# A two-block transformer kernel: the first weight in two halves, buffer clears off GpSimd, another order on VectorE

## The reference

```python
def reference(x, ...):
    # block 1
    h = rms_norm(x, attn_pre_g);  proj = h @ w_in            # 1024 -> 2304
    y_a = rms_norm(sliding_window_attention_with_sinks(...)) # 8 query heads, 2 key heads, ALiBi
    y_b = differential_attention(...)                        # 4 heads, two softmaxes each, lambda
    x = x + rms_norm(concat(y_a, y_b) @ w_out, attn_post_g)
    u = rms_norm(x, ffn_pre_g) @ w_up                        # 1024 -> 8192, then a causal 3-tap convolution
    x = x + rms_norm((gelu(c_gate) * c_value) @ w_down, ffn_post_g)
    # block 2, modulated by mod = silu(c) @ w_ada + b_ada    # 1024 -> 6144
    x = x + gate_mix * (concat(dilated_mixture, stick_breaking) @ w_out_2)
    x = x + gate_ffn * hierarchical_moe(...)                 # 32 experts, top 2
    return rms_norm(x, g_final)
```

## Time and profile before

| | |
|---|---|
| median of 3 runs | 1101.72 us (1100.43 to 1105.70) |
| the profiled execution | 1104.06 us; its span in the trace 1102.4 us |
| TensorE busy | 1017.5 us, 92% |
| VectorE busy | 541.0 us, 49% |
| ScalarE busy | 324.1 us, 29% |
| GpSimd busy | 80.8 us, 7% |
| HBM read | 310.32 MB, 282 GB/s over the span |
| the chain that ended last | TensorE 82%, VectorE 11%, waits for nothing shown 2%, ScalarE 2%, DMA 2% |

### The profile page before, as it was taken

How to read it: one execution, slowest core, us unless ns; L and a number is a source line. 1 busy time by engine, 2 the same in 40 slices (tenths; PEclk the granted TensorE clock), 3 DMA queues, 4 the chain that set the end, 5 groups by cost and what they waited for, 6 DMA issues and landing times.

```text
span 1102.4 us, 15139 instructions
## 1 busy us (share of the span) xinstructions
PE 1017.5 (92%) x5949; PEld 707.5 (64%) x5951; DVE 541.0 (49%) x903; ACT 324.1 (29%) x501; POOL 80.8 (7%) x111
## 2 busy tenths in 40 slices
PE   2998759999999999999988899999999999999995
PEld 2997649998999998889877544444444444433441
DVE  6556786979999996738674411111111111111113
ACT  3354516435445464527450100000000000000001
POOL 7300030101111000200010000000000000000000
PEclk9999779999999999899989899999999999999998
DMA  7316045788988864244335799799999999999991
GB/s 272 121 40 217 13 154 183 253 282 285 343 297 291 312 251 168 77 160 147 137 154 200 319 432 375 323 367 424 430 425 427 426 427 429 423 426 429 427 409 41
DMA packets 60351, 311.89 MB, mean 283 GB/s; under 512 B 4005, under 2 KB 5370, under 8 KB 47514
## 3 DMA queue, kind: packets, MB, share of 16 engines
q1 hardware_dynamic: 51728, 284.17, 65.6%
q0 software_dynamic: 7456, 26.91, 6.6%
q10 hardware_dynamic: 1130, 0.29, 0.1%
HBM read 310.32 MB, written 1.05 MB: 282 GB/s over the span
## 4 chain that ended last, share of the span: by engine, by line
PE 82%; DVE 11%; issue 2%; ACT 2%; DMA 2%; POOL 0%; DVEq 0%; POOLq 0%; SPq 0%; ACTq 0%
PE bank L741 12%; PE bank L742 11%; PE bank L743 11%; PE bank L1112 10%; PE bank L1081 10%; PE bank L1072 10%; PE bank L1023 6%; PE bank L1036 5%; DVE ring_r L1499 4%; DMA ring<-in_w_up 1%; PE bank L795 1%; PE bank L826 1%; ACT scratch L1394 1%; PE bank L731 1%; PE bank L1090 1%
## 5 line engine op out<-in xcount | busy, mean ns | idle before, releaser
L741 PE MATMUL bank<-hT_r,ring_r 128*128 128x256 f32 x744 | 215.8, 290 | 14.8 <-DVE ring_r L1499 12.7
L743 PE MATMUL bank<-hT_r,ring_r 128*128 128x256 f32 x744 | 213.0, 286 | 0.0
L1499 DVE TENSOR_TENSOR ring_r<-ring,ring_r 128x2048 fp32r<-128x2048 f32 (+1 forms) x78 | 173.7, 2262 | 18.7 <-ACT ring_r L1183 18.4
L741 PEld LDWEIGHTS bank<-hT_r,ring_r 128*128 128x128 f32 x744 | 145.3, 195 | 18.2 <-issue 16.4
L1183 ACT ACTIVATE ring_r<-ring 128x2048 fp32r<-128x2048 f32 (+1 forms) x78 | 144.1, 1890 | 43.5 <-DMA ring<-in_w_up 36.4
L742 PE MATMUL bank<-v_tok_r,ring_r 128*128 128x256 f32 x512 | 145.6, 284 | 0.0
L743 PEld LDWEIGHTS bank<-hT_r,ring_r 128*128 128x128 f32 x744 | 145.3, 195 | 0.0
L1949 DVE TENSOR_TENSOR scratch<-scratch,bank 128x512 f32<-128x512 f32 x16 | 11.0, 688 | 237.0 <-PE bank L1081 237.0
L1081 PE MATMUL bank<-ring,scratch 128*64 128x512 f32 x496 | 113.3, 595 | 0.0
L1112 PE MATMUL bank<-ring,scratch 128*64 128x512 f32 x480 | 106.3, 595 | 6.6 <-ACT scratch L1394 6.6
L1072 PE MATMUL bank<-ring,scratch 128*64 128x512 f32 x480 | 105.6, 592 | 0.0
(11 more groups left out here) (292 smaller groups left out, 1427.9 us busy)
## 6 DMA issues: line engine op xcount, KB each, us to landing
ring<-in_w_up SPq DMA_DIRECT2D x47, 2048.0 KB, 12.2
ring<-in_w_down SPq DMA_DIRECT2D x37, 2048.0 KB, 10.9
ring<-in_w_gate SPq DMA_DIRECT2D x30, 2048.0 KB, 12.6
ring<-in_w_in SPq DMA_DIRECT2D x10, 2048.0 KB, 8.3
kT<-in_w_ada POOLq DMA_DIRECT2D x24, 512.0 KB, 8.2
ring<-in_w_out SPq DMA_DIRECT2D x4, 2048.0 KB, 8.2
scratch<-in_w_ada POOLq DMA_DIRECT2D x12, 512.0 KB, 6.5
final_g<-in_w_ada POOLq DMA_DIRECT2D x12, 512.0 KB, 7.9
```

What stands on the lines that cost most here:

```text
L741: pe.matmul(dst, lhs[0], rhs[0], start=start, stop=False, **flags)
L743: return pe.matmul(dst, lhs[1], rhs[0], start=False, stop=stop, **flags)
L1499: last = ve.tensor_tensor(lo, raw, hi, ALU.subtract)
```

## The change

1. The first piece of w_in is loaded as two halves of four row blocks, the first with a semaphore of its own (`s_first`). VectorE counts `s_wlo_first` when the first half is split. TensorE goes through items 0 to 3 with the first four row blocks, then through the same items with the last four (`project_first`), where before it did each item with all 8 blocks.
2. ScalarE now writes all 8 rounded input blocks of the first projection, and VectorE only the low parts, after it has split the weight's first half.
3. TensorE transposes the constants between the two tiles of tokens instead of after them.
4. The five small loads of sinks and lambda vectors move from ScalarE's queue to SyncE's, behind the first piece, and SyncE doesn't wait for any small load any more.
5. `qz` is cleared by VectorE, first of all. `ada` is cleared by ScalarE in two halves of 3072 columns, by a copy of a column times zero, each between two sums of squares.
6. The computation of `lncount` is cut in two. The first eight operations (`multiplicity`) come before VectorE's last copy ahead of the attention; the others stay where they were, with one copy more.
7. At the output projection VectorE splits the first FFN piece (N_FFN) between the two tiles' normalisations instead of before both.
8. GpSimd issues the modulation loads before its small clears for block two (`SB_ADD`, `SB_NEG`) instead of after them.

```diff
@@ SyncE
-            for c in range(IN_CHUNKS):
-                if c == 1:
-                    sp.wait_ge(s_stage, 16 * 12)
-                    sp.wait_ge(s_lamv, 16 * 4)
-                    sp.wait_ge(s_sink, 16)
+            raw = chunk_view(0)
+            for half, done in enumerate((s_first, loaded[0])):
+                tiles_of_half = slice(half * KD // 2, (half + 1) * KD // 2)
+                sp.dma_start(raw[:, tiles_of_half, :], w_in[:, tiles_of_half, 0:HALF]).then_inc(done, 16)
+            sp.dma_start(sinks, a["swa_sinks"][0].partition_broadcast(P)).then_inc(s_sink, 16)
+            for n, name in enumerate(("diff_lq1", "diff_lk1", "diff_lq2", "diff_lk2")):
+                sp.dma_start(lamv[:, n, :], a[name][0].partition_broadcast(P)).then_inc(s_lamv, 16)
+            for c in range(1, IN_CHUNKS):
                 straight(N_IN + c, w_in[:, :, c * HALF:min((c + 1) * HALF, w_in.shape[2])])
@@ GpSimd
             inverse_roots(T)
-            pool.memset(qz[:, :, :], 0.0).then_inc(s_qzero, 1)
             then(pool.memset(from_here[:, :], 1.0))
...
             inverse_roots(3 * T)
 
-            pool.wait_ge(s_src["mix1"], T)
-            then(pool.memset(ada, 0.0))
+            pool.wait_ge(s_adaz, 2)
             pool.dma_start(ada[0:1, :], a["b_ada_2"]).then_inc(s_ada0, 16)
+
+            pool.wait_ge(s_sq[0], 2 * T)
...
 
             then(pool.memset(SB_ADD, 0.0))
@@ TensorE
             pe.wait_ge(s_const, 1)
-            turn("attn1", hn)
+            turn("attn1", hn, range(T - 1))
 
             pe.wait_ge(s_stage, 16 * 12)
             pe.transpose(PS[7][:, 0:P], stage[:, 0, :], ident[:, :])
             pe.transpose(PS[7][:, P:2 * P], stage[:, 1, :], ident[:, :])
             pe.transpose(PS[7][:, 2 * P:2 * P + 53], stage[0:53, 2, :], ident[0:53, 0:53]).then_inc(s_vecT, 1)
+            turn("attn1", hn, range(T - 1, T))
             pe.wait_ge(s_vec, 1)
-            for n in range(AHEAD[0]):
+
+            def project_first(count):
+
+                w = split_view(N_IN % LANES)
+                for half in range(2):
+                    pe.wait_ge(*((s_wlo_first, 1), (s_wlo, N_IN + 1))[half])
+                    for n in range(count):
+                        c, kind, where = items1[n]
+                        assert c == 0 and kind == "q" and n < AHEAD[0]
+                        for k in range(half * KD // 2, (half + 1) * KD // 2):
+                            if n == 0:
+                                pe.wait_ge(s_hT["attn1"], k + 1)
+                            last = product(item_bank(0, n)[:, 0:S], both(w, k, where[1], P), tiles("attn1", k),
+                                           start=(k == 0), stop=(k == KD - 1))
+                        if half == 1:
+                            last.then_inc(s_gemm[0], 1)
+
+            project_first(4)
+            for n in range(4, AHEAD[0]):
                 project(0, N_IN, n)
@@ ScalarE
             def split_one(n, part, more=0):
-                if part == 0:
+                if n == N_IN and part == 0:
+                    sc.wait_ge(s_first, 16)
+                elif n == N_IN or part == 0:
                     sc.wait_ge(loaded[n % LANES], 16 * (n // LANES + 1) + 16 * more)
...
                                   scale=D ** -0.5, accum_out=sq[:, 2 * t + c:2 * t + c + 1]).then_inc(s_sq[m], 1)
+                    if c == 0 and cleared is not None:
+                        sc.activation(cleared, zero, ACT.Copy, scale=0.0).then_inc(s_adaz, 1)
...
-            rounded("attn1", lambda k: vec[:, 2, R_PRE + k:R_PRE + k + 1], first=KD // 2)
+            rounded("attn1", lambda k: vec[:, 2, R_PRE + k:R_PRE + k + 1])
...
+            zero = ident[:, P - 1:P].broadcast_to([P, ADA // 2])
             for t in range(T):
-                squares(0, t, s_proj[0])
+                squares(0, t, s_proj[0], ada[:, t * (ADA // 2):(t + 1) * (ADA // 2)], zero)
@@ VectorE
+            ve.memset(qz[:, :, :], 0.0).then_inc(s_qzero, 1)
             for t in range(T):
                 ve.wait_ge(s_x[t], 16)
                 ask_root(mean_squares(x[:, t, :], mix[:, t, :], column()))
...
-            low("attn1", lambda k: vec[:, 2, R_PRE + k:R_PRE + k + 1], mine=KD // 2)
-            split(N_IN)
+            split_one(N_IN, 0)
+            low("attn1", lambda k: vec[:, 2, R_PRE + k:R_PRE + k + 1])
+            split_one(N_IN, 1)
             split(N_IN + 1)
...
-            take(0, range(3, AHEAD[0]))
+            take(0, range(3, AHEAD[0] - 1))
+            ve.wait_ge(s_const, 7)
+            multiplicity()
+            take(0, range(AHEAD[0] - 1, AHEAD[0]))
             ve.wait_ge(s_mask, 1)
...
-            then(ve.tensor_scalar(dist, negdist[:, :], -1.0, None, ALU.mult))
...
-            then(ve.tensor_tensor(lncount[:, :], lncount[:, :], term, ALU.add))
+            log_of_multiplicity()
             for h in range(DIL_H):
                 last = ve.scalar_tensor_tensor(bias[:, h, :], negdist[:, :], float(np.float32(dil_slopes[h])),
                                                lncount[:, :], ALU.mult, ALU.add)
             then(last)
-            split(N_FFN)
             ve.wait_ge(s_rows, 32)
             for t in range(T):
                 post_norm(0, post_attn, t)
                 norm("ffn", t, hn)
+                if t == 0:
+                    split(N_FFN)
```

More of the change, by code:

```diff
@@ L684, in _ @@
             inverse_roots(3 * T)
-            pool.wait_ge(s_src["mix1"], T)
-            then(pool.memset(ada, 0.0))
+            pool.wait_ge(s_adaz, 2)
             pool.dma_start(ada[0:1, :], a["b_ada_2"]).then_inc(s_ada0, 16)
+            pool.wait_ge(s_sq[0], 2 * T)
+            w_ada = a["w_ada_2"].rearrange("o (k p) n -> p (o k) n", p=P)
+            with pool.Fori(0, ADA // ADA_W) as r:
+                for c in range(ADA_EACH):
+                    pool.wait_ge(s_sum, 2 * (ADA_EACH * r + c) + 2)
+                    pool.dma_start(ada_buf[c % ADA_BUFS], w_ada[:, c, ds(ADA_W * r, ADA_W)])\
+                        .then_inc(s_adab[c % ADA_BUFS], 16)
             then(pool.memset(SB_ADD, 0.0))
@@ L724, in _, with turn @@
         def _(pe):
-            def turn(tag, src):
-                for t in range(T):
+            def turn(tag, src, tiles_of_tokens=range(T)):
+                for t in tiles_of_tokens:
                     pe.wait_ge(s_src[tag], t + 1)
@@ L1165, in scaled, with rounded @@
                                   scale=scale(k), bias=0.0 if shift is None else shift(k)).then_inc(s_hTA, 1)
-            def rounded(tag, scale, shift=None, first=0):
-                for k in range(first, KD):
+            def rounded(tag, scale, shift=None):
+                for k in range(KD):
                     sc.wait_ge(s_turn[tag], k // 2 + 1)
@@ L1463, in scaled, with low @@
                     ins.then_inc(s_hT[tag], 1)
[L1465 removed]
+            def low(tag, scale, shift=None):
                 dst = lo_T[tag]
[L1468 to L1471 removed]
                 for k in range(KD + 1):
[L1473 to L1476 removed]
+                    if k < KD:
+                        ve.wait_ge(s_hhi[tag], k // 2 * 2 + 2)
                     if k < KD:
@@ L1501, in split_one @@
                     last.then_inc(s_wlo, 1)
+                elif n == N_IN:
+                    last.then_inc(s_wlo_first, 1)
             def take(blk, pieces):
```

73 lines of the change are left out of this document (31 added, 42 removed).

## The result

The changed kernel takes **1097.07 us** (median of 7 runs, 1094.98 to 1098.71), the kernel before 1103.09 in the same comparison (1100.43 to 1106.23). The ratio is 0.9938, 95% interval 0.9917 to 0.9959: 6.8 us faster, where 14.5 were forecast, and 2 us above the range. Timed again on another chip (12 runs) the ratio was 0.9951 (0.9931 to 0.9971).

The account below looks back on a forecast made before the run. TensorE's holes at the front and behind the first output projection were taken as the bound, with VectorE's scalings held by GpSimd's clears; -7.9 - 6.6 = -14.5 us, from 1101.72 to 1087.2, range 1081 to 1095.

Parts of the forecast that it names:

- Part B: Behind the first output projection: last scaling freed of GpSimd's clear, ending at 154.9 against 161.53 us, -6.6 us.
- Part A: Front up to the first attention score: first score at 40.6 against 48.52 us, -7.9 us.
- (1) to (3): Front: clear on VectorE off the path, constants ready at 12.5 us, TensorE's first product at 15.2 against 25.44.
- (4): Front: second weight, queued at about 5 us, lands at 18 to 21, split by 25 to 26, hidden.
- (5): Front: VectorE becomes the later; third weight's rounding at about 28.7 us, eight small operations 2.9, first score at 39.6.
- (6): Front: GpSimd's two long bias-table operations meet VectorE at about 29 to 37 us, costing 1.0; first score 40.6.
- R1: Lock goes both ways: third weight's subtractions and eight operations wait for long GpSimd operations, 4.8 not 1.0; 1091; chance 0.13.
- R2: More clock: TensorE's first products at the upper level, at most 2.1 us, 1.6 more behind the projection; 1083 to 1085; chance 0.12.
- As a block: Whole kernel: what is won at either hole moves everything behind it earlier by the same amount, up to the end.
- R4: Gain taken back downstream by the expert stage's DMA stream, half given back; 1094.5; chance 0.06.
- R3: Long scalings are not the clears' doing and stay long; -9.6 us in all, 1092; chance 0.03.
- R5: Front slower: small loads starve beside 5 MB of weights, constants and splits wait, 8.2 slower, 1109.9; chance 0.02.

Follow-up runs that it names:

- run 3: The kernel before with only the part behind the output projection: ada cleared by ScalarE, FFN piece split between the two tiles; 1098.35 us, 0.9954.
- run 5: The changed kernel with ada's clear back on GpSimd and the FFN split ahead of both tiles, front kept as changed; 1102.88 us, 0.9995 of before.
- run 6: The changed kernel with multiplicity operations in an attention gap, small loads on ScalarE's queue, selections waiting for the second weight's split; 1089.69 us, 0.988 of before.
- run 4: The changed kernel with GpSimd's two long selections waiting until VectorE has split the second weight; 1095.96 us, 0.9925 of before.
- run 9: The kernel of run 6 plus 20 unread products filling TensorE's pause ahead of the first score; 1088.86 us, 0.986 of before.
- run 8: The kernel of run 1 once more, with no further edit, for a second trace; 1092.76 us.
- run 10: The kernel of run 6 without the selections' wait for the second weight's split; 1092.88 us, 0.9902 of before.
- run 1: The changed kernel with all multiplicity operations back at the output projection; 1094.61 us, 0.9914 of before.
- run 2: The changed kernel with the five small loads back on ScalarE's queue, SyncE still not waiting for them; 1096.65 us, 0.9933 of before.
- runs 7: The changed kernel once more with no edit, giving its second trace; 1098.22 us, 0.9951 of before.

## Why the prediction was wrong

**Part B was right** in mechanism and size: 12.2 us became 5.6 (-6.6 forecast and read), and alone, without the eight operations' move, it gave 0.9954, 5.1 us (2.8 to 7.3; run 3's forecast was 5.1). **Part A was wrong**: -7.9 us forecast, -0.6 measured (run 5; -2.5 to +1.3), and 1.7 us of what run 5 holds belong to part B. By its steps:

(1) to (3) held. The clear took 3.47 us (3.0 to 4.6), constants were ready at 12.65 (12.5), the first product came at 15.40 (15.2).

(4) failed by a little: the second weight was rounded from 22.77 (22.21 in the second trace) and not by 21. I let 2 MB follow at the full rate; the DMA share falls to 0.14 at 12 to 14 us and 0.34 at 14 to 16 while the five small loads, which stand in the same queue, land 9.3 to 11.6 us after their issue. On ScalarE's queue (run 6) the share doesn't go below 0.67 there, and the rounding starts at 21.7, still late.

(5) missed a chain. "The third weight's rounding stands behind the copy of item 2, about 28.7" leaves out that the lambda's exponential stands ahead of it on ScalarE's queue, and waits for the lambda product, which stands behind the second weight's subtractions on VectorE. That couples the third weight to the second. Where no selection meets the second weight's subtractions or the lambda product, that rounding still starts at 31.08 (run 4), 2.4 us late, and with the second weight in earlier at 30.56 (run 6), with the third weight's subtractions ending at 38.05, not 35.2. The eight small operations cost their 2.9 us as forecast (42.99 to 45.85).

(6) failed most in the first trace: I priced the meeting with the two long selections at 1.0 us, and placed it at 29 to 37 us, on the third weight's subtractions and the eight small operations. It came at 25.5, on the second's, and it was rival R1: 2.7 us on the subtractions (7.17 less 4.49) and 1.75 on the lambda product, 4.4 of its 4.8, on other instructions than R1 named, and passed on whole by that chain. In the second trace it was 0.2 and 2.6, 2.8 us. The row I went by, subtractions of 2.3 us beside GpSimd's small operations, showed only the order in which VectorE comes first. The mean of 2.6 us hid what happened on the other side: singly, the four GpSimd operations took 4.82, 2.34, 2.34 and 0.84 us, and the first of them waited out two subtractions.

The Trainium skill ("SBUF — State Buffer", Who interferes with whom) says that a VectorE instruction with two SBUF inputs contends with a GpSimd one that reads SBUF, and that the one issued first keeps the other out. I held that the trace didn't bear it out; the 7.17 against 4.69 us of one kernel's two traces do.

**The clock** was named only as a gain (R2). At the first products that gain came in part: TensorE passed 12 of them at the lower level, before it had been 27. Behind the pause it was a loss, which the sum had at nothing: the scores take 3.75 us instead of 2.02, and the attention, first score to last scaling, 74.8 us instead of 72.0 (74.2 in the second trace; run 9, without the pause: 72.0). The pause ahead of the scores and their length, trace by trace: 0.61 and 2.02 us before, 1.67 and 3.58 in run 8, 2.48 and 3.49 in run 6, 4.56 and 3.75 in the changed kernel.

**"As a block"** held in most runs. Lead at the end of the last scaling before the FFN, by the trace, and gain in the median: 5.3 and 5.1 us (run 3), 11.0 and 10.8 (run 10), 14.2 and 13.2 (run 6), 15.6 and 15.4 (run 9), 10.4 and 9.5 (run 1), 10.3 and 8.3 (run 4). It did less well in run 2 (11.2 and 7.4) and run 5 (3.0 and 0.6), and two single traces can lie 3 us off it (runs 7 and 8). So R4, half of the gain taken back downstream, is not needed; whether a smaller part is taken back stays open. R3 and R5 are out: the scalings are short, and the constants were ready at 12.65.

**The sum.** In the first trace the first score came 5.9 us later than forecast (46.45 against 40.6): 3.4 from the meeting with the selections beyond the 1.0 allowed (6), and 2.4 from the second weight and the chain behind it (4, 5). The clock took 2.7 more during the attention. Together that is 8.6 us, more than the 7.9 forecast. In the second trace the same terms are 1.8, 2.0 and 2.2, together 5.9. Between the two lie the times: 14.5 forecast and 6.1 measured, as the mean of both comparisons (0.9945), are 8.4 us apart.

The runs show what undoing single edits gives, which is another question. Against 0.9945 the multiplicity operations are worth 3.4 us (run 1), the wait of the selections 2.4 (run 10 against run 6) and the small loads' queue 1.3 (run 2): 7.1 together, and run 6, with all three edits, is 7.2 better. With 3 to 4 us as the interval of each such difference, the 7.2 stands clear, the first share barely, and the other two not. Of these three the multiplicity operations are no part of the miss, for step (5) had paid for them: by the forecast's own steps run 6 should have had its first score at 37.7 (40.6 less 2.9), and it came at 39.54, late by the chain of step (5).

## What to carry to other kernels

When a stall goes, walk each engine's queue behind it again, and ask of every long GpSimd instruction which two-input VectorE one it will meet at its new time, in both orders. An instruction of 0.2 us between two engines' queues can carry a stall of several. Price a pause of TensorE with the slower stretch behind it, and take two traces of one kernel before a difference of 2 us between two kernels is explained.

## What the runs showed of the hardware

- Two traces of the same kernel differ by 2.1 us at the first score and by 3.4 us at the end, in opposite directions. The first is the order in which VectorE and GpSimd met; of the 6.0 us between a lead of 2.6 at 152 us and a lag of 3.4 at the end, the granted clock accounts for 1.7, and the rest is not explained.
- Where a GpSimd selection of 3072 columns (2.83 us alone) stood against VectorE instructions with both inputs in SBUF, the one that came second waited: a subtraction took 4.91 us instead of 2.28, a product of 64 columns 2.84 instead of 0.21, the selection itself 4.23.
- The granted clock fell to 0.50 in the middle of the FFN's last products, where the records show TensorE busy without a break, in some executions and not in others.
- Twenty unread products in a pause of 2.5 us kept the clock at its upper level and shortened the first attention by 1.5 us (73.5 to 72.0).
- A clear of 4096 fp32 columns takes VectorE 3.47 us and GpSimd 3.51; 3072 take ScalarE 2.77.
